# Last phase of a decoder block on one core: each full-height matmul replaced by two of 64 rows into separate banks

## The chip, the cores and the metric

One core of one Trainium2 chip runs the whole program. The metric is the device time of one execution in microseconds (us), the median of several runs. Below, a *product* is one matmul of TensorE whose moving operand has 512 columns (or the two half-height ones that take its place), and a *unit* is 256 rows by 512 columns of a weight matrix (512 KB): two tiles of 128 rows, used with two blocks of 128 tokens in three passes, so 12 products.

## The reference

One layer of a hybrid block: x (256 tokens, width 2048, float32) is RMS-normalised and projected by one wide matrix (2048 x 18432) to the inputs of two token mixers, a retention and a differential attention, and their gates. Then:

```
o_ret  = rmsnorm(retention(rq, rk, rv)) * silu(rz)
o_diff = rmsnorm(diff_attention(dq, dk, dv)) * (1 - lam_init) * silu(dz)
mixed  = sigmoid(g_ret) * (o_ret @ w_ret_up) + sigmoid(g_diff) * (o_diff @ w_diff_up)
h      = x + mixed @ w_out
out    = rmsnorm(h) * final_norm_w
```

All of it is float32. The last phase, which the change concerns, is `o_diff @ w_diff_up`, the merge into `mixed`, `mixed @ w_out`, the sum with x and the final norm.

## The kernel before

**Products.** Float32 accuracy comes from splitting each operand into a rounded part (`_hi`) and a remainder (`_lo`), both of the type fp32r, and adding three passes: hi x hi, hi x lo, lo x hi (`three_passes`, lines 1218 to 1224). The activations are the stationary operand (128 rows of the contraction by 128 tokens), the weights are the moving one (128 rows by 512 columns). A group is 512 output columns for both token blocks: 8 units, 16 contraction tiles, accumulated in two banks of PSUM (one for each token block). `start_group` waits until both banks have been drained.

**The stream of weights.** Units are numbered through the whole program; the ring for them has 4 slots. For each unit SP loads it into `raw` (line 397), when the slot's last remainder has been computed; ScalarE rounds it into `w_hi` (line 562), when TensorE is done with the slot; VectorE subtracts, giving `w_lo` (line 806); TensorE waits for both at the start of the unit (`units_split`). ScalarE and VectorE run three units ahead, in loops over `s` written out by hand: at each step first the split of unit s + 3, then whatever else the step has.

**Last phase.** 64 units: four groups g = 0 to 3 with `w_diff_up` and `ot` as the stationary operand, then four groups g = 4 to 7 with `w_out` and `xt`. `tail_banks` gives the groups banks 2, 3 and 0, 1 by turns. At the first step behind each of the groups 0 to 3 VectorE runs `merge_diff` (line 1092): it multiplies the gate by each bank (line 1098) and adds that to `mixed` (line 1102). One step later it transposes the two results in squares of 32 (line 821); SP moves the strips with 8 DMAs (`turn`, line 405), which stand in its queue ahead of a load of weights; three steps later ScalarE rounds the result into `xt_hi` (line 759) and VectorE takes the remainder `xt_lo` (line 1115). TensorE needs the last quarter of that operand at the seventh unit (u = 6) of group 4, line 1334. Behind the last rounding ScalarE issues two loads, x again into `gate` and the final norm's weights into `zs` (lines 780, 781). Behind each of the groups 4 to 6 VectorE adds the banks to x (`add_residual`, line 1123), the first time after waiting for these loads; the split of the unit follows behind it in the queue at the next step. ScalarE squares and sums the rows, GpSimd multiplies by the final weights.

**The end.** In the last group the last four units are taken block by block (line 1341), so that block 0's final chain (add, squares, reciprocal root on GpSimd, scaling, store) runs under block 1's products, and block 1's stands behind them.

**The start.** TensorE's program begins with nine semaphore increments (line 1179), then waits for a tile of ones and runs nine warm-up matmuls on it (line 1251), then the first products, `tile_by_pass` (line 1188). The first unit comes in halves of one tile each: ScalarE rounds the second half at line 639.

Of the kernel before, what the change touches and what calls it, by code (L numbers as in the profile page):

```python
# [31 lines left out]
P = 128  # L32
# [13 lines left out]
AHEAD = 3  # L46
GROUPS_D = D // COLS
HALF = COLS // 2

QK = 128  # L50
V = 256
# [29 lines left out]
SQUARE = 32  # L81
STRIPS = P // SQUARE
TURN = 16 * STRIPS
WARM_UPS = 9
TURN_LAG = AHEAD + RING + 1


# [52 lines left out]
def diff_uses_high(it, j):  # L140
    return it * 4 + (9 + j)
# [14 lines left out]

def tail_uses_low(j):
    return 19 + j


def tail_banks(g):

    return 2 - 2 * (g % 2)
# [8 lines left out]
def build(nc, x, x_t, norm_w, w_in, w_ret_up, w_diff_up, w_out, lambda_q1, lambda_k1, lambda_q2,  # L172
# [5 lines left out]
    with ExitStack() as ctx:  # L178
# [3 lines left out]
        def sem(name):  # L182
            return ctx.enter_context(nc.semaphore(name))
# [106 lines left out]
        mt_hi_ready = sem("mt_hi_ready")  # L290
        x_again = sem("x_again")
        h_ready = sem("h_ready")
        h_squared = sem("h_squared")
        h_weighted = sem("h_weighted")
        h_norm_step = sem("h_norm_step")
# [10 lines left out]
        def lam_row(i):  # L306

            return gate[:, 1, i * P:(i + 1) * P]

        def attn_of(a):  # L310

# [485 lines left out]
        def _(dve):  # L797
# [294 lines left out]
            def merge_diff(j):  # L1092

                group_done(U_TAIL + (j + 1) * UNITS - 1)
                cols = slice(j * COLS, (j + 1) * COLS)
                banks = tail_banks(j)
                for b in range(BLOCKS):
                    dve.tensor_tensor(gate[:, b, cols], gate[:, b, cols], bank[banks + b][:, :], ALU.mult) \
                       .then_inc(drained[banks + b], 1)
                for b in range(BLOCKS):  # L1100
                    dve.wait_ge(drained[banks + b], tail_uses_low(j // 2) + 1)
                    dve.tensor_tensor(mixed[:, b, cols], mixed[:, b, cols], gate[:, b, cols], ALU.add) \
                       .then_inc(mixed_ready, 1)
# [15 lines left out]
            def add_residual(j, b):  # L1119

                cols = slice(j * COLS, (j + 1) * COLS)
                bk = tail_banks(j) + b
                dve.tensor_tensor(gate[:, b, cols], gate[:, b, cols], bank[bk][:, :], ALU.add).then_inc(h_ready, 1)  # L1123

                dve.wait_ge(h_ready, 2 * j + b + 1)
                dve.sem_inc(drained[bk], 1)

            for s in range(FIRST, 2 * GROUPS_D * UNITS):
                if U_TAIL + s + AHEAD < U_END:
# [46 lines left out]

        @block.tensor
        def _(pe):
            pe.sem_inc(units_done, RING)
            for b in range(8):  # L1180
                pe.sem_inc(filled[b], 1)

            def start_group(banks, uses):

                for b in range(BLOCKS):
                    pe.wait_ge(drained[banks + b], uses)
# [31 lines left out]
            def three_passes(s, u, kk, bk, b, left_hi, left_lo):  # L1218

                k = u * KU + kk  # L1220
                hi, lo = left_hi[:, k, b * P:(b + 1) * P], left_lo[:, k, b * P:(b + 1) * P]
                pe.matmul(bank[bk][:, :], hi, w_hi[:, s, kk, :], start=k == 0, stop=False)  # L1222
                pe.matmul(bank[bk][:, :], hi, w_lo[:, s, kk, :], start=False, stop=False)  # L1223
                return pe.matmul(bank[bk][:, :], lo, w_hi[:, s, kk, :], start=False, stop=k == KT - 1)  # L1224

            def keys_by_v(dst, a, x, b, v_col, start, stop):

                hi, lo = keys_hi(a)[:, x * P:(x + 1) * P], keys_lo(a)[:, x * P:(x + 1) * P]
                cols = slice(v_col, v_col + V)
                pe.matmul(dst, hi, v_hi[:, b, cols], start=start, stop=False)  # L1230
                pe.matmul(dst, hi, v_lo[:, b, cols], start=False, stop=False)  # L1231
                return pe.matmul(dst, lo, v_hi[:, b, cols], start=False, stop=stop)  # L1232
# [12 lines left out]
                pe.matmul(dst, left_hi[:, m, left], right_lo[:, m, right], start=False, stop=False)  # L1245
                return pe.matmul(dst, left_lo[:, m, left], right_hi[:, m, right], start=False, stop=True)  # L1246


            pe.wait_ge(ones_ready, 1)
            for i in range(WARM_UPS):  # L1250
                pe.matmul(bank[7][:, 0:P], ones[:, :], ones[:, :], start=True, stop=True)  # L1251

            for it in range(RET_ITS):
                n0 = it * (RET_G * UNITS) + U_RET
# [71 lines left out]
            for s in range(2 * GROUPS_D * UNITS - RING):  # L1326
                g, u = s // UNITS, s % UNITS
                banks = tail_banks(g)
                if u == 0:
                    start_group(banks, tail_uses_low(g // 2))  # L1330
                if g == 0 and u in (0, 6):
                    pe.wait_ge(ot_lo_ready, 2 * HEADS - 2 + 2 * (u // 6))
                if g == GROUPS_D and u in (0, 6):
                    pe.wait_ge(mt_lo_ready, 2 * GROUPS_D - 2 + 2 * (u // 6))
                if g < GROUPS_D:
                    unit(U_TAIL + s, u, banks, ot_hi, ot_lo)
                else:
                    unit(U_TAIL + s, u, banks, xt_hi, xt_lo)


            for b in range(BLOCKS):
                for u in range(UNITS - RING, UNITS):
                    if b == 0:
                        pe.wait_ge(units_split, 2 * (U_END - UNITS + u + (RING + 1)))
                    for kk in range(KU):
                        mm = three_passes(u % RING, u, kk, tail_banks(GROUPS_D - 1) + b, b, xt_hi, xt_lo)
                mm.then_inc(filled[tail_banks(GROUPS_D - 1) + b], 1)


# [53 lines left out]
```

## Time and profile before

| | |
|---|---|
| median of 3 runs | 1092.63 us (1092.34 to 1092.67) |
| the profiled execution | 1092.4 us |
| its span in the profile | 1090.6 us |
| mean granted TensorE clock | 0.997 of full speed |
| busy: matmuls / weight loads / VectorE / ScalarE / GpSimd | 1080.7 / 900.1 / 686.7 / 528.1 / 47.2 us |

PE is TensorE's matmul row, PEld its loads of the stationary operand (they overlap matmuls), DVE is VectorE, ACT ScalarE, POOL GpSimd, SP SyncE; a q behind a name is the engine's sequencer, where DMAs are issued. The profile's matmul rows give a length of 0.39 us for a product, but products follow each other faster than that, since they are pipelined and their ends are modelled: their pace is read from the starts. L1222 is line 1222 of the kernel. In a row of the timeline, what stands in brackets is the idle time of the engine before it and what ended it.

### The profile page before, as it was taken

How to read it: one execution, taken by the hardware profiler on the slowest of the kernel's cores; microseconds unless marked ns; L12 is line 12 of the kernel's file. 1: busy time of each engine (PE TensorE's matmuls, PEld its weight loads, DVE VectorE, ACT ScalarE, POOL GpSimd, SP SyncE). 2: the span in 40 equal slices, each digit the busy share in tenths (PEclk: the TensorE clock that was granted, in tenths of full speed). 3: DMA queues.
4: the chain of work that ended last, by engine and by line, in shares of the span. 5: the costliest groups of instructions: out<-in, count | busy, mean ns of one | idle time of the engine just before them, and what ended most of it. 6: DMA issues, size and time to landing. Idle time of an engine off the chain costs nothing.

```text
span 1090.6 us, 13145 instructions
## 1 busy us (share of the span) xinstructions
PE 1080.7 (99%) x4890; PEld 900.1 (83%) x4890; DVE 686.7 (63%) x848; ACT 528.1 (48%) x689; POOL 47.2 (4%) x63
## 2 busy tenths in 40 slices
PE   9999999999999999999999999999999999999997
PEld 7888888888888888888888888888888888888885
DVE  6675575485566455566766767576757676676554
ACT  6554455344455433344654464446544554444443
POOL 0100000000000000000100002000200020000111
PEclk9999999999999999999999999999999999999998
DMA  9877667666667655667566766766677666666862
GB/s 326 305 245 219 182 196 209 193 199 209 193 181 212 201 195 194 192 179 245 167 216 186 219 200 196 213 200 196 205 209 213 195 205 201 208 211 211 323 213 101
DMA packets 141072, 227.97 MB, mean 209 GB/s; under 512 B 14416, under 2 KB 40784, under 8 KB 140240
## 3 DMA queue, kind: packets, MB, share of 16 engines
q1 hardware_dynamic: 140448, 223.98, 66.3%
q10 hardware_dynamic: 560, 3.15, 0.7%
q8 instruction: 38, 0.62, 0.2%
q14 instruction: 26, 0.21, 0.1%
HBM read 210.84 MB, written 2.10 MB: 195 GB/s over the span
## 4 chain that ended last, share of the span: by engine, by line
PE 99%; issue 1%; DVE 0%; POOL 0%; ACT 0%; ACTq 0%; POOLq 0%; DVEq 0%
PE bank L1222 31%; PE bank L1223 31%; PE bank L1224 31%; PE bank L1232 1%; PE bank L1231 1%; PE bank L1230 1%; PE bank L1251 0%; PE bank L1194 0%; PE bank L1198 0%; PE bank L1201 0%; PE bank L1313 0%; PE bank L1246 0%; PE bank L1245 0%; PE bank L1244 0%; PE bank L1270 0%
## 5 line engine op out<-in xcount | busy, mean ns | idle before, releaser
L806 DVE TENSOR_TENSOR w_lo<-raw,w_hi 128x1024 fp32r<-128x1024 f32 x380 | 471.0, 1244 | 372.1 <-ACT w_hi L562 371.0
L562 ACT ACTIVATE w_hi<-raw 128x1024 fp32r<-128x1024 f32 x380 | 402.9, 1061 | 521.4 <-PE bank L1224 487.8
L1222 PE MATMUL bank<-w_hi,xt_hi 128*128 128x512 f32 x1264 | 493.1, 390 | 0.0
L1224 PE MATMUL bank<-w_hi,xt_lo 128*128 128x512 f32 x1264 | 491.9, 389 | 0.0
L1223 PE MATMUL bank<-w_lo,xt_hi 128*128 128x512 f32 x1264 | 491.8, 389 | 0.0
L1224 PEld LDWEIGHTS bank<-w_hi,xt_lo 128*128 128x128 f32 x1264 | 237.3, 188 | 49.6
L1222 PEld LDWEIGHTS bank<-w_hi,xt_hi 128*128 128x128 f32 x1264 | 237.3, 188 | 48.8
L1223 PEld LDWEIGHTS bank<-w_lo,xt_hi 128*128 128x128 f32 x1264 | 237.4, 188 | 48.5
L1222 PE MATMUL bank<-w_hi,ot_hi 128*128 128x512 f32 x256 | 99.6, 389 | 0.0
L1223 PE MATMUL bank<-w_lo,ot_hi 128*128 128x512 f32 x256 | 99.6, 389 | 0.0
L1224 PE MATMUL bank<-w_hi,ot_lo 128*128 128x512 f32 x256 | 99.6, 389 | 0.0
L1222 PEld LDWEIGHTS bank<-w_hi,ot_hi 128*128 128x128 f32 x256 | 48.0, 188 | 10.0
L1223 PEld LDWEIGHTS bank<-w_lo,ot_hi 128*128 128x128 f32 x256 | 48.0, 188 | 10.0
L1224 PEld LDWEIGHTS bank<-w_hi,ot_lo 128*128 128x128 f32 x256 | 48.0, 188 | 9.9
L531 POOL TENSOR_TENSOR zs<-zs,sub 128x512 f32<-128x512 f32 x8 | 14.1, 1787 | 498.9 <-DVE zs L871 498.9
L842 DVE TENSOR_TENSOR rot<-rot 128x512 f32<-128x512 f32 x24 | 16.6, 693 | 2.5
L821 DVE STREAM_TRANSPOSE squares_t<-rot 128x512 f32<-128x512 f32 x24 | 17.1, 711 | 0.8
L541 POOL TENSOR_TENSOR mixed<-gate,zs 128x512 f32<-128x512 f32 x6 | 10.6, 1788 | 160.0 <-DVE gate L1123 160.0
L516 POOL TENSOR_TENSOR ms<-ss,eps_sb 128x2 f32<-128x2 f32 x16 | 5.1, 322 | 279.8 <-ACT junk L596 279.8
L833 DVE TENSOR_TENSOR rot<-bank,rope_sb 128x512 f32<-128x512 f32 x24 | 16.4, 683 | 0.6 <-POOL rope_sb L510 0.6
L836 DVE TENSOR_TENSOR rot<-bank,rope_sb 128x512 f32<-128x512 f32 x24 | 16.3, 679 | 0.0
L738 ACT ACTIVATE probs<-probs,neg_max 128x256 f32<-128x256 f32 (+1 forms) x32 | 14.1, 443 | 0.7 <-DVE neg_max L1054 0.7
(112 smaller groups left out, 474.8 us busy)
## 6 DMA issues: line engine op xcount, KB each, us to landing
raw<-w_in_dram SPq DMA_DIRECT2D x284, 512.0 KB, 4.3
raw<-w_ret_up_dram SPq DMA_DIRECT2D x32, 512.0 KB, 3.6
raw<-w_diff_up_dram SPq DMA_DIRECT2D x32, 512.0 KB, 4.5
raw<-w_out_dram SPq DMA_DIRECT2D x32, 512.0 KB, 4.5
rot<-squares_t SPq DMA_DIRECT2D x96, 64.0 KB, 2.4
zs<-squares_t SPq DMA_DIRECT2D x48, 64.0 KB, 2.2
normed<-squares_t SPq DMA_DIRECT2D x48, 64.0 KB, 2.2
raw<-w_in_dram SPq DMA_DIRECT2D x8, 256.0 KB, 5.3
```

What stands on the lines that cost most here:

```text
L531: pool.tensor_tensor(z, z, sub08[:, :].unsqueeze(1).broadcast_to([P, 2, V]), ALU.mult) \
L562: act.activation(w_hi[:, s, :, :], raw[:, s, :, :], ACT.Copy).then_inc(hi_ready, 1)
L738: last = act.activation(p, p, ACT.Exp, bias=neg_max[:, a, j:j + 1], accum_out=row_sum[:, a, j:j + 1])
L806: dve.tensor_tensor(w_lo[:, s, :, :], raw[:, s, :, :], w_hi[:, s, :, :].bitcast(F32), ALU.subtract) \
L821: dve.transpose(to, src).then_inc(squares_ready[slot], 1)
L833: dve.tensor_tensor(rot[:, 0, :].rearrange("p (g d) -> p g d", d=64), src[:, :].rearrange("p (g d) -> p g d", d=64), cos, ALU.mult) \
L836: dve.tensor_tensor(rot[:, 1, :].rearrange("p (m s d) -> p m s d", s=2, d=64), src[:, :].rearrange("p (m s d) -> p m s d", s=2, d=64)[:, : ...
L842: dve.tensor_tensor(rot[:, 0, :], rot[:, 0, :], rot[:, 1, :], ALU.add).then_inc(rot_ready, 1)
L1222: pe.matmul(bank[bk][:, :], hi, w_hi[:, s, kk, :], start=k == 0, stop=False)
L1223: pe.matmul(bank[bk][:, :], hi, w_lo[:, s, kk, :], start=False, stop=False)
L1224: return pe.matmul(bank[bk][:, :], lo, w_hi[:, s, kk, :], start=False, stop=k == KT - 1)
L1230: pe.matmul(dst, hi, v_hi[:, b, cols], start=start, stop=False)
```

## The change

In the last phase each product becomes two (`row_halves`): the lower 64 rows of both operands into the banks 0 to 3 as before, the upper 64 rows into the bank four further up (`UPPER`), one after the other in TensorE's program. The two partial sums are added by VectorE: in `merge_diff` the lower bank is copied to SBUF, the upper is added, and the gate is multiplied by that; in `add_residual` the two banks are added one after the other. Each of these steps waits for the one before it. The banks 4 to 7, which the last phase did not use before, are guarded by `tail_uses_upper`. Separately, the warm-up matmuls are eight instead of nine and stand ahead of the nine increments. No other phase is changed.

```diff
-WARM_UPS = 9
+WARM_UPS = 8
+HALF_P = P // 2
+UPPER = 4
...
+def tail_uses_upper(g):
+    return diff_uses_high(DIFF_ITS - 1, 4) + g // 2 if g % 2 == 0 else 1 + g // 2
...
+        def rows_sum(b):
+            return probs[:, b * COLS:(b + 1) * COLS]
...
@@ merge_diff
                 for b in range(BLOCKS):
-                    dve.tensor_tensor(gate[:, b, cols], gate[:, b, cols], bank[banks + b][:, :], ALU.mult) \
+                    dve.tensor_copy(rows_sum(b), bank[banks + b][:, :]).then_inc(row_sums, 1)
+                    dve.wait_ge(row_sums, 4 * j + 2 * b + 1)
+                    dve.tensor_tensor(rows_sum(b), rows_sum(b), bank[UPPER + banks + b][:, :], ALU.add).then_inc(row_sums, 1)
+                    dve.wait_ge(row_sums, 4 * j + 2 * b + 2)
+                    dve.sem_inc(drained[UPPER + banks + b], 1)
+                    dve.tensor_tensor(gate[:, b, cols], gate[:, b, cols], rows_sum(b), ALU.mult) \
                        .then_inc(drained[banks + b], 1)
...
@@ add_residual
-                dve.tensor_tensor(gate[:, b, cols], gate[:, b, cols], bank[bk][:, :], ALU.add).then_inc(h_ready, 1)
+                dve.tensor_tensor(gate[:, b, cols], gate[:, b, cols], bank[bk][:, :], ALU.add).then_inc(h_lower, 1)
+                dve.wait_ge(h_lower, 2 * j + b + 1)
+                dve.sem_inc(drained[bk], 1)
+                dve.tensor_tensor(gate[:, b, cols], gate[:, b, cols], bank[UPPER + bk][:, :], ALU.add).then_inc(h_ready, 1)
 
                 dve.wait_ge(h_ready, 2 * j + b + 1)
-                dve.sem_inc(drained[bk], 1)
+                dve.sem_inc(drained[UPPER + bk], 1)
...
@@ tensor engine
+            pe.wait_ge(ones_ready, 1)
+            for i in range(WARM_UPS):
+                pe.matmul(bank[7][:, 0:P], ones[:, :], ones[:, :], start=True, stop=True)
+
             pe.sem_inc(units_done, RING)
             for b in range(8):
                 pe.sem_inc(filled[b], 1)
...
+            def row_halves(s, u, kk, bk, b, left_hi, left_lo):
+
+                k = u * KU + kk
+                tokens = slice(b * P, (b + 1) * P)
+                for left, right, first, last in ((left_hi, w_hi, k == 0, False), (left_hi, w_lo, False, False),
+                                                 (left_lo, w_hi, False, k == KT - 1)):
+                    pe.matmul(bank[bk][:, :], left[0:HALF_P, k, tokens], right[0:HALF_P, s, kk, :], start=first, stop=last)
+                    mm = pe.matmul(bank[UPPER + bk][:, :], left[HALF_P:P, k, tokens], right[HALF_P:P, s, kk, :], start=first,
+                                   stop=last)
+                return mm
+
+            def unit_by_rows(n, u, banks, left_hi, left_lo):
+
+                pe.wait_ge(units_split, 2 * n + (2 * RING + 2))
+                for kk in range(KU):
+                    for b in range(BLOCKS):
+                        mm = row_halves(n % RING, u, kk, banks + b, b, left_hi, left_lo)
+                mm.then_inc(units_done, 1)
...
-            pe.wait_ge(ones_ready, 1)
-            for i in range(WARM_UPS):
-                pe.matmul(bank[7][:, 0:P], ones[:, :], ones[:, :], start=True, stop=True)
...
                 if u == 0:
                     start_group(banks, tail_uses_low(g // 2))
+                    start_group(UPPER + banks, tail_uses_upper(g))
...
                 if g < GROUPS_D:
-                    unit(U_TAIL + s, u, banks, ot_hi, ot_lo)
+                    unit_by_rows(U_TAIL + s, u, banks, ot_hi, ot_lo)
                 else:
-                    unit(U_TAIL + s, u, banks, xt_hi, xt_lo)
+                    unit_by_rows(U_TAIL + s, u, banks, xt_hi, xt_lo)
...
-                        mm = three_passes(u % RING, u, kk, tail_banks(GROUPS_D - 1) + b, b, xt_hi, xt_lo)
+                        mm = row_halves(u % RING, u, kk, tail_banks(GROUPS_D - 1) + b, b, xt_hi, xt_lo)
```

## Rows read from the trace of the kernel before

**Rows 1.** The page, busy us of each engine (share of the span) and instructions.

```profile
PE 1080.7 (99%) x4890; PEld 900.1 (83%) x4890; DVE 686.7 (63%) x848; ACT 528.1 (48%) x689; POOL 47.2 (4%) x63
```

**Rows 2.** The page, the chain that ended last, by engine.

```profile
PE 99%; issue 1%; DVE 0%; POOL 0%; ACT 0%; ACTq 0%; POOLq 0%; DVEq 0%
```

**Rows 3.** Windows: busy us of each engine (instructions), in two stretches of the phase.

```profile
915.00:1000.00 85.00, 85.00 (x376) 70.38 (x375) 53.98 (x60) 36.39 (x38) 0.00 (x0) 1.00 0.65 213
1000.00:1083.00 83.00, 82.89 (x366) 68.32 (x364) 45.78 (x50) 35.36 (x45) 11.14 (x7) 1.00 0.59 209
```

**Rows 4.** Timeline (start us, length us), last phase, two products 12 apart.

```profile
950.13 0.39 PE L1222 MATMUL bank<-w_hi,ot_hi 128*128 128x512 f32 x1
...
952.85 0.39 PE L1222 MATMUL bank<-w_hi,ot_hi 128*128 128x512 f32 x1
```

**Rows 5.** Timeline of TensorE's matmuls, products of 256 columns, five apart.

```profile
894.31 0.28 PE L1230 MATMUL bank<-v_hi,ot_hi 128*128 128x256 f32 x1
...
894.91 0.28 PE L1232 MATMUL bank<-v_hi,ot_lo 128*128 128x256 f32 x1
```

**Rows 6.** Timeline of the start, the first real products.

```profile
5.99 0.93 PE L1194 MATMUL bank<-w_hi,xt_hi 128*128 128x512 f32 x2
6.49 0.63 ACT L639 ACTIVATE w_hi<-raw 128x512 fp32r<-128x512 f32 x1 [1.46 <-DMA raw<-w_in_dram]
...
7.45 0.41 PEld L1194 LDWEIGHTS bank<-w_hi,xt_hi 128*128 128x128 f32 x2
```

**Rows 7.** Timeline of the end, last group.

```profile
1077.49 0.69 DVE L1123 TENSOR_TENSOR gate<-gate,bank 128x512 f32<-128x512 f32 x1 [2.78 <-PE bank L1224]
...
1078.37 0.43 DVE L1158 CUSTOM_DVE_ANT_0 mixed<-gate 128x256 f32<-128x256 f32 x1 [0.18 <-DVE gate L1123]
...
1080.03 0.49 DVE L1172 TENSOR_SCALAR mixed<-mixed,h_rstd 128x512 f32<-128x512 f32 x1 [0.73 <-POOL h_rstd L545]
...
1082.51 0.39 PE L1224 MATMUL bank<-w_hi,xt_lo 128*128 128x512 f32 x1
1082.93 0.69 DVE L1123 TENSOR_TENSOR gate<-gate,bank 128x512 f32<-128x512 f32 x1 [1.75 <-PE bank L1224]
```

**Rows 8.** Timeline of the weight loads, where products have 128 columns.

```profile
865.06 0.54 PEld L1313 LDWEIGHTS bank<-zs,left_whole 128*128 128x128 f32 x4
865.52 0.19 PEld L1222 LDWEIGHTS bank<-w_hi,xt_hi 128*128 128x128 f32 x1
```

**Rows 9.** Timeline of VectorE, last phase.

```profile
968.88 1.23 DVE L806 TENSOR_TENSOR w_lo<-raw,w_hi 128x1024 fp32r<-128x1024 f32 x1 [0.24 <-ACT w_hi L562]
...
998.20 1.28 DVE L1098 TENSOR_TENSOR gate<-gate,bank 128x512 f32<-128x512 f32 x2
...
1000.60 1.22 DVE L806 TENSOR_TENSOR w_lo<-raw,w_hi 128x1024 fp32r<-128x1024 f32 x1
...
1009.92 1.29 DVE L1115 TENSOR_TENSOR xt_lo<-rot,xt_hi 128x512 fp32r<-128x512 f32 x2 [0.76 <-ACT xt_hi L759]
...
1024.18 1.52 DVE L1123 TENSOR_TENSOR gate<-gate,bank 128x512 f32<-128x512 f32 x2 [2.92 <-DMA zs<-final_norm_w_dram]
1025.92 1.81 DVE L806 TENSOR_TENSOR w_lo<-raw,w_hi 128x1024 fp32r<-128x1024 f32 x1 [0.22 <-DVE gate L1123]
```

**Rows 10.** Timeline of TensorE's matmuls, the first products of three units.

```profile
973.93 0.39 PE L1222 MATMUL bank<-w_hi,ot_hi 128*128 128x512 f32 x1
...
1012.01 0.39 PE L1222 MATMUL bank<-w_hi,xt_hi 128*128 128x512 f32 x1
...
1028.33 0.39 PE L1222 MATMUL bank<-w_hi,xt_hi 128*128 128x512 f32 x1
```

**Rows 11.** Timeline of ScalarE and its queue, behind the last rounding.

```profile
1009.50 0.39 ACTq L780 DMA_DIRECT2D gate<-x_dram  x1
```

**Rows 12.** The chain that ended last at the start (start us, us, what).

```profile
0.93 1.23 issue
2.16 4.18 PE bank L1251 x18
```

More of the change, by code:

```diff
@@ L292, in build @@
         h_ready = sem("h_ready")
+        h_lower = sem("h_lower")
+        row_sums = sem("row_sums")
         h_squared = sem("h_squared")
```

## The prediction

> **What bounds the kernel now.** Four views, in this order. The page's busy shares: TensorE's matmul row is at 99% of the span [rows 1], but the ends of matmuls are modelled, so this alone says little. The chain that ended last is 99% TensorE and 1% issue [rows 2]: the array is the bound, everywhere. The windows over the last phase (64 units of 12 products, 768 in all) show matmuls filling 85.00 of 85.00 us and 82.89 of 83.00, VectorE at 54.0 and 45.8 [rows 3]: VectorE has room on average, TensorE has none. The timeline then gives the period of a product: the one at 950.13 and the one at 952.85 are 12 apart, 2.72 us, 0.2267 each [rows 4]. Products of 256 columns follow each other by (894.91 - 894.31) / 5 = 0.120 us [rows 5]. The 256 further columns cost 0.1067 us, so 512 cost 0.2133, and each change of the stationary operand about 13.3 ns, whatever the width. Work that is not hidden by products lies at the two ends only: 5.99 us before the first real one [rows 6], and 1090.6 - (1082.51 + 0.39) = 7.7 us behind the last one's end [rows 7].
>
> **1. The 768 products become 1536 of half height.** Their arithmetic doesn't shrink: each half still streams 512 columns, 0.2133 us. All that can be won is the 13.3 ns, 768 x 0.0133 = 10.2 us, and only if one half's change hides under the other half's stream, and the other way round, without lengthening the period of either. Against this: each half is a chain of its own (stream, change, stream), and its period stays 0.2133 + 0.0133 however the other one is placed in time. Two such chains side by side end when one does. I take no change, 0.2267 us for a pair.
>
> Bound below: 0.2133, that is -10.2 us. Bound above: the loads, of which each pair needs two. Where products are narrow (128 columns) loads set the pace: four take 0.54 us from the first's start to the last's end, one 0.19, so they start (0.54 - 0.19) / 3 = 0.117 us apart [rows 8]. Two loads one after the other are 0.233 us, against the 0.2267 that hide them: the cover that was wide (one load in 0.2267) is used up. At 0.233 a pair costs 6.7 ns more, 5.1 us over 768. The far bound: the halves do not run side by side at all, 768 x 0.2267 = +174 us. The nearest rows, the periods and the loads, lie within 6% of 0.2267 on both sides; that value is taken.
>
> A rule of the Trainium skill speaks against the change here: "TensorE: Matmul & The Clock Gate", section "LDWEIGHTS (loading the stationary operand)", has the load's time go by columns and not by rows, so a load of 64 rows costs what one of 128 does. By its figure, an estimate of 107 ns each, two would just fit under a product, and the sum would stay as it is. No load of 64 rows is in this trace. "TensorEngine Tiling (Array Packing)", section "Tiling Modes", speaks for the change: tiles load and multiply independently. By it the halves do run side by side, and perhaps their loads too; the trace of before shows neither.
>
> **2. VectorE's merge, four times.** Before: two multiplications from the banks and two additions, from 998.20 to the next operation's start at 1000.60, 2.40 us, 0.60 apiece, since they overlap [rows 9]. After, per block: copy, wait, add the upper bank, wait, multiply. A step that needs the one before it starts 0.88 us after it (1077.49 to 1078.37 [rows 7]), against 0.60 for an independent one. The copy from a bank is not in the trace: its nearest rows are the 0.49 us scaling [rows 7] and the multiplication from a bank, 1.28 - 0.60 = 0.68 us [rows 9]; I take the latter, which reads a bank too. A block costs 0.88 + 0.88 + 0.60 = 2.36 instead of 0.60, +1.76 (1.35 to 1.8 with a short copy and short waits); two blocks, rounded down, +3.4 us (2.7 to 3.6).
>
> Behind it, in the same queues, stand the transpositions, the eight DMAs of the turn on SP, ScalarE's rounding, VectorE's remainder, and the splits of the next units' weights. The path is one line, so all of it comes 3.4 us later.
> - After the second merge, the split of unit 24 ended at 968.88 + 1.23 = 970.1 [rows 9]; TensorE starts that unit at 973.93 [rows 10]. 3.4 later it still fits, by 0.4. After the first and the third, where the turn's DMAs land sooner, more than 1 us is left. Cost nothing.
> - After the fourth, the output product needs the last quarter of its stationary operand at its unit 6. That remainder was ready at 1009.92 + 1.29 = 1011.2 [rows 9]; unit 6 starts at 1012.01 [rows 10]. Slack 0.8. With +3.4 it is there at 1014.6: TensorE waits **2.6 us** (1.9 to 2.8).
> - ScalarE issues the reload of x and of the final weights behind its rounding, at 1009.50 [rows 11]; they go 3.4 us later. The residual sum of the first output group waits for them until 1024.18 (VectorE idle 2.92), and behind it in VectorE's queue the split of unit 12 of the output product ends at 1025.92 + 1.81 = 1027.7 [rows 9], with the unit at 1028.33 [rows 10]. Slack 0.6.
>
> **3. The residual sum, four times.** Four additions, two of them dependent, instead of two. Before, two take 1025.92 - 1024.18 = 1.74 us with their waits [rows 9], so +1.75. For the first group this adds to the late reload: 3.4 + 1.75 - 0.6 = 4.5 us late at unit 12, of which 2.6 are waited already. The reload (3072 KB in 14.7 us, with some four weight transfers of 512 KB among it) now meets one of these fewer, since SP sends it ahead: up to 1.5 us at that rate, of which I take 0.5. Both waits together **4.0 us** (2.5 to 5.0). The later groups don't wait for a reload: nothing.
>
> **4. The end.** The second block's chain of the last group starts behind TensorE's last product, with the addition at 1082.93 [rows 7]. One more dependent addition stands in it: **+0.9 us** (0.7 to 0.9). The first block's chain was at its scaling at 1080.03, with one operation to go; 0.9 later it is still out of the way.
>
> **5. The start.** The nine increments ahead of the warm-up stand in 1.23 us of issue between 0.93 and 2.16, and the 18 records of warm-up take 4.18 us, 0.23 apart against 0.117 for the same shape later [rows 8, 12]: half clock. They hold the first real product until 5.99. Freed, and one warm-up (2 records, 0.46 us) shorter, TensorE could start at about 4.7. But the second half's rounding runs from 6.49 to 7.12, and TensorE came to it at 7.45 already [rows 6]: **-0.3 us**. The other way: if the array stayed at half clock up to 1.5 us longer than it did, 3 to 4 products more at twice the period, +0.8. Nobody waits for the increments, which now lie under the warm-up, before 7 us.
>
> **Sum.** The profiled execution took 1092.4 us (1.8 outside the span of 1090.6): 0 + 4.0 + 0.9 - 0.3 = +4.6, 1097.0. The median of the runs shown, 1092.63, is 0.2 above it and gives 1097.2; I say 1097. The case's own range is 1095 to 1099.5.
>
> **Rivals.**
> A. *The change of operand hides.* For: the excess is the same at 512 and 256 columns, so it may sit in something that the other half can use the time of. Against: the argument of the two chains. Price: the waits above are set by VectorE and count from the start of the output product, so unit 12 comes at the same time whatever the period: the 12 units before it save nothing, 52 x 12 x 0.0133 = 8.3 us is saved, less 0.9 at unit 24, whose slack of 0.4 goes when eight units run 1.3 us faster. 1097.2 - 8.3 + 0.9 = 1089.8. It gives "faster" when over nine tenths of the excess vanish, or when the waits are at their low end.
> B. *Loads set the pace*, 0.233 us a pair: 52 x 12 x 0.0067 = +4.2 us, 1101.4. For: the spacing of loads. Against: those loads waited for products as well, and might go closer.
> C. *The halves run partly or not side by side*, the change doesn't do what it says: from 0.25 us a pair (52 x 12 x 0.0233 = +14.6, 1111.8) to one after the other (1267). For: no row shows two products in the array from different rows. Against: only that it would be possible.
> D. *VectorE's extra time is covered.* Were the merge only 0.8 us longer there would be no wait at all, and the sum is +0.6, 1093.2. Against: three operations can't take the time of one.
>
> **Chances.** Forecast 0.36, A 0.30, B 0.12, C 0.13, D 0.09. A measurement of this kernel can tell some 0.2% from no change, 2.2 us: 1090.4 to 1094.8. A is 0.20 faster and 0.10 within; D 0.02 faster and 0.07 within; 0.04 of the forecast is within. Faster 0.22, same 0.21, slower 0.57. The range 1087.5 to 1106 leaves out C and the far end of A.
>
> **What would show it.** The period of a pair in the timeline: 0.227 is the forecast, 0.213 to 0.216 A, 0.233 B, more C. A gap in TensorE ahead of the seventh unit of the output product, with mt's remainder at its end, about 2.6 us, and one before unit 12, about 1.4: steps 2 and 3; neither: D. VectorE from the merge's first operation to the split behind it: 5.8 us instead of 2.4. From TensorE's last product to the end: 0.9 more. First real product at 4.7, second tile at 7.1 to 7.2: step 5. The forecast is wrong if a pair's period is off by over 4 ns, or if no wait stands at unit 6.

## The result, and the profile after

The changed kernel takes **1103.03 us** (median of 4 runs, 1101.64 to 1103.64) against 1092.58 for the kernel before in the same measurement: a ratio of 1.0094, 95% interval [1.0082, 1.0106]. It is slower, as forecast, and inside the wide range (1087.5 to 1106), but outside the 1095 to 1099.5 that the forecast gave for its own case: it loses 10.4 us where the forecast of 1097 meant 4.4. The profiled execution took 1101.64 us with a span of 1099.8, so span against span the change cost 9.2 us, and that is the difference which the traces can take apart. The last phase's 64 units are numbered 0 to 63 here; a group has eight. The output product starts at unit 32, so its "unit 6" and "unit 12" are units 38 and 44. The fourth merge stands behind group 3, and its place is told from the start of unit 32.

First the page: busy us of each engine, and the chain that ended last [rows 1, 2].

```profile
PE 1084.9 (99%) x5656; PEld 903.4 (82%) x5656; DVE 703.4 (64%) x872; ACT 529.0 (48%) x689; POOL 44.5 (4%) x63
```

```profile
PE 91%; DMA 3%; DVE 2%; SPq 1%; issue 1%; ACT 1%; ACTq 0%; POOLq 0%; POOL 0%; DVEq 0%
```

TensorE's share hardly moved, but its part of the chain fell from 99% to 91%: the path to the end now leaves the array for a DMA, VectorE and SyncE's queue. The busy line would not have told that.

**The period.** TensorE and its loads in the timeline (start, length), one product and the two behind it [rows 4]:

```profile
959.72 0.39 PE L1257 MATMUL bank<-w_hi,ot_hi 64*128 64x512 f32 x1
959.73 0.39 PE L1258 MATMUL bank<-w_hi,ot_hi 64*128 64x512 f32 x1
...
960.18 0.39 PE L1257 MATMUL bank<-w_hi,ot_lo 64*128 64x512 f32 x1
...
960.18 0.18 PEld L1257 LDWEIGHTS bank<-w_hi,ot_hi 64*128 64x128 f32 x1
960.18 0.18 PEld L1258 LDWEIGHTS bank<-w_hi,ot_hi 64*128 64x128 f32 x1
...
960.40 0.39 PE L1257 MATMUL bank<-w_hi,ot_hi 64*128 64x512 f32 x1
```

A pair every (960.40 - 959.72) / 3 = 0.2267 us, as before to the last digit. The two halves start within 0.01 us of each other, and so do their two loads: the loads are not one after the other, which rival B needed. The Trainium skill ("TensorE: Matmul & The Clock Gate", section "The mechanism") has the products of tiles in different rows start about 4 ns apart and their loads run beside products in flight; the trace agrees, with 0.01 us between the halves in the rows above. A load of 64 rows takes 0.18 us here, one of 128 rows 0.19 [rows 8]. In the Trainium skill (same page, section "LDWEIGHTS (loading the stationary operand)") the time of a load goes by its columns and not by its rows; the trace agrees, though these rows are longer than the 107 ns that the prediction estimated from that page.

**VectorE in the fourth merge** [rows 9], timeline:

```profile
1000.64 0.68 DVE L1111 COPY probs<-bank 128x512 f32<-128x512 f32 x1
1001.36 0.69 DVE L1113 TENSOR_TENSOR probs<-probs,bank 128x512 f32<-128x512 f32 x1
1002.19 0.69 DVE L1116 TENSOR_TENSOR gate<-gate,probs 128x512 f32<-128x512 f32 x1
...
1006.16 1.22 DVE L819 TENSOR_TENSOR w_lo<-raw,w_hi 128x1024 fp32r<-128x1024 f32 x1
```

The merge lasts from 1000.64 to 1006.16, 5.52 us instead of 2.40: +3.12, where +3.4 was forecast. But it also *starts* late: 1000.64 against 998.20 before, 2.44 us, of which TensorE's own schedule explains only 0.60 (unit 32 starts at 996.29, before at 995.69). It begins 4.35 us behind the start of unit 32 instead of 2.51. That 1.84 is nobody's price in the forecast.

**TensorE at the two waits** [rows 10], timeline:

```profile
1017.59 0.79 PE L1257 MATMUL bank<-w_hi,xt_hi 64*128 64x512 f32 x1 [4.42 <-DVE xt_lo L1133]
...
1018.61 0.63 PE L1257 MATMUL bank<-w_hi,xt_lo 64*128 64x512 f32 x1
1019.03 0.63 PE L1257 MATMUL bank<-w_hi,xt_hi 64*128 64x512 f32 x1
...
1036.61 0.50 PE L1257 MATMUL bank<-w_hi,xt_hi 64*128 64x512 f32 x1 [0.84 <-DVE w_lo L819]
```

Unit 38 starts 7.30 us after unit 37 instead of 2.72. Behind the wait the pairs come 0.42 us apart, not 0.227: the windows over that stretch (columns: window, its length, busy us of PE, PEld, DVE, ACT, POOL, granted clock, DMA share, GB/s) show why.

```profile
1017.60:1021.00 3.40, 3.40 (x16) 2.74 (x18) 1.34 (x2) 1.13 (x2) 0.00 (x0) 0.51 1.04 399
1021.10:1024.50 3.40, 3.40 (x33) 2.81 (x31) 2.16 (x2) 1.06 (x1) 0.00 (x0) 1.00 1.00 407
```

A granted clock of 0.51 is the lower of the two levels. It lasts 3.4 us behind an idle stretch of 4.42, and unit 38 takes 1.67 us longer for it (4.39 instead of 2.72).

**The chain through unit 12** (start, us, what), from the turn behind the fourth merge to TensorE [rows 11 for the reload]:

```profile
1007.30 0.72 DVE squares_t L834
1008.08 0.55 SPq L418
...
1012.57 2.92 DMA rot<-squares_t
...
1015.78 0.39 ACTq L793
1016.19 14.69 DMA zs<-final_norm_w_dram
1030.90 0.70 DVE gate L1141
...
1034.31 2.25 DVE w_lo L819
1036.61 0.50 PE bank L1257
```

Read it as one line: transposition, eight DMAs, their landing, ScalarE's issue of the reload, 14.7 us of transfer, the residual sum, the split, TensorE. Nothing in it is the array. A delay of the fourth merge arrives at unit 12 in full, less the slack of 0.6, as long as the transfers behind it keep their lengths.

**ScalarE behind the first turn**, timeline. These rows show how lateness is handed on:

```profile
947.09 1.16 ACT L772 ACTIVATE xt_hi<-rot 128x512 fp32r<-128x512 f32 x2 [4.46 <-DMA rot<-squares_t]
...
950.25 1.06 ACT L575 ACTIVATE w_hi<-raw 128x1024 fp32r<-128x1024 f32 x1 [1.05 <-DMA raw<-w_diff_up_dram]
951.58 1.06 ACT L575 ACTIVATE w_hi<-raw 128x1024 fp32r<-128x1024 f32 x1 [0.27 <-DMA raw<-w_diff_up_dram]
952.85 1.06 ACT L575 ACTIVATE w_hi<-raw 128x1024 fp32r<-128x1024 f32 x1 [0.21 <-DMA raw<-w_diff_up_dram]
```

VectorE next to it:

```profile
951.41 3.83 DVE L819 TENSOR_TENSOR w_lo<-raw,w_hi 128x1024 fp32r<-128x1024 f32 x3 [0.89 <-ACT w_hi L575]
955.16 0.69 DVE L1111 COPY probs<-bank 128x512 f32<-128x512 f32 x1
```

ScalarE stands 4.46 us before the strips (1.33 in the trace of before), then waits for weights; three roundings come close together, VectorE splits three units in a row, and only then can the second merge begin. In the trace of before ScalarE had caught up with the array by then and waited for it. The four merges start 0.1, 0.5, 2.0 and 2.4 us later than before.

The chain that ended last (start, us, what) shows the same links further on, from the second merge's transposition to the fourth merge:

```profile
961.82 0.72 DVE squares_t L834
...
968.84 4.59 DMA raw<-w_diff_up_dram
...
973.51 1.07 ACT w_hi L575
...
985.10 0.72 DVE squares_t L834
...
991.64 5.32 DMA raw<-w_out_dram
...
997.05 1.07 ACT w_hi L575
...
999.50 1.23 DVE w_lo L819
1000.72 0.61 DVE probs L1111
```

The transposition lets the turn's DMAs go. The load behind them in SyncE's queue lands and is rounded, three splits run in a row, and the third merge starts right behind the last of them, as VectorE's timeline has it:

```profile
974.68 3.84 DVE L819 TENSOR_TENSOR w_lo<-raw,w_hi 128x1024 fp32r<-128x1024 f32 x3 [0.78 <-ACT w_hi L575]
978.43 0.68 DVE L1111 COPY probs<-bank 128x512 f32<-128x512 f32 x1
```

The merge lasts to 983.96, a split follows, and the third transposition stands at 985.10; behind its turn comes the next load, and behind the splits of that one the fourth merge. None of these steps is TensorE's. (Between 977.24 and 985.10 the profile's own chain goes by another load and leaves 0.54 us unexplained; the merge and the split fill that time on VectorE.)

**End and start.** VectorE at the end [rows 7], and TensorE's products at the start of the first unit's two tiles [rows 6]:

```profile
1091.34 0.69 DVE L1141 TENSOR_TENSOR gate<-gate,bank 128x512 f32<-128x512 f32 x1 [0.91 <-PE bank L1258]
1092.17 0.69 DVE L1144 TENSOR_TENSOR gate<-gate,bank 128x512 f32<-128x512 f32 x1
```

```profile
4.92 1.19 PE L1219 MATMUL bank<-w_hi,xt_hi 128*128 128x512 f32 x2 [0.16 <-ACT w_hi L647]
...
7.41 0.66 PE L1219 MATMUL bank<-w_hi,xt_hi 128*128 128x512 f32 x2
```

The first six products follow each other at 0.42 us here, (7.41 - 4.92) / 6, and before at 0.28 (the second tile's first product stood at 7.67): of the 1.07 us by which the first product starts earlier, 0.26 are left at the second tile.

The ledger, from the starts of the units' first products:

| where | before | after | costs |
|---|---|---|---|
| start of unit 0 | 908.65 | 908.57 | -0.08 |
| unit 0 to 32: first change to half height 0.16, small waits 0.52 | 87.04 | 87.72 | +0.68 |
| unit 32 to 44 | 32.64 | 40.32 | +7.68 |
| unit 44 to the last product (0.13 behind the wait) | 54.18 | 54.30 | +0.12 |
| last product to the end of the span | 8.09 | 8.92 | +0.83 |
| span | 1090.6 | 1099.8 | +9.2 |

### The profile page after: what moved, and what is told of

Read it like the earlier page. It is cut to its first block, busy times and chain, and to the rows that moved or that the text cites. A ratio compares the mean times of both kernels' runs of the same rounds, so it can differ in the third digit from the quotient of the medians.

```text
span 1099.8 us, 14725 instructions
## 1 busy us (share of the span) xinstructions
PE 1084.9 (99%) x5656; PEld 903.4 (82%) x5656; DVE 703.4 (64%) x872; ACT 529.0 (48%) x689; POOL 44.5 (4%) x63
## 4 chain that ended last, share of the span: by engine, by line
PE 91%; DMA 3%; DVE 2%; SPq 1%; issue 1%; ACT 1%; ACTq 0%; POOLq 0%; POOL 0%; DVEq 0%
PE bank L1249 26%; PE bank L1248 26%; PE bank L1247 26%; PE bank L1257 9%; DMA zs<-final_norm_w_dram 1%; SPq L418 1%; DMA raw<-w_diff_up_dram 1%; DVE w_lo L819 1%; PE bank L1276 1%; PE bank L1275 1%; PE bank L1274 1%; DMA raw<-w_out_dram 0%; PE bank L1219 0%; ACT w_hi L575 0%; PE bank L1223 0%
## 5 line engine op out<-in xcount | busy, mean ns | idle before, releaser
L1247 PE MATMUL bank<-w_hi,xt_hi 128*128 128x512 f32 x1136 | 443.3, 390 | 0.0
L1248 PE MATMUL bank<-w_lo,xt_hi 128*128 128x512 f32 x1136 | 442.0, 389 | 0.0
L1257 PE MATMUL bank<-w_hi,xt_hi 64*128 64x512 f32 x128 | 50.5, 395 | 5.3 <-DVE xt_lo L1133 4.4
L1258 PE MATMUL bank<-w_hi,xt_hi 64*128 64x512 f32 x128 | 50.6, 395 | 0.0
L1257 PE MATMUL bank<-w_lo,xt_hi 64*128 64x512 f32 x128 | 50.0, 391 | 0.0
L1258 PE MATMUL bank<-w_lo,xt_hi 64*128 64x512 f32 x128 | 50.0, 391 | 0.0
L1258 PE MATMUL bank<-w_hi,xt_lo 64*128 64x512 f32 x128 | 49.9, 390 | 0.0
L1257 PE MATMUL bank<-w_hi,xt_lo 64*128 64x512 f32 x128 | 49.9, 390 | 0.0
L1247 PE MATMUL bank<-w_hi,ot_hi 128*128 128x512 f32 x128 | 49.8, 389 | 0.0
L1248 PE MATMUL bank<-w_lo,ot_hi 128*128 128x512 f32 x128 | 49.8, 389 | 0.0
L1249 PE MATMUL bank<-w_hi,ot_lo 128*128 128x512 f32 x128 | 49.8, 389 | 0.0
L1258 PE MATMUL bank<-w_hi,ot_hi 64*128 64x512 f32 x128 | 49.8, 389 | 0.0
L1257 PE MATMUL bank<-w_hi,ot_hi 64*128 64x512 f32 x128 | 49.8, 389 | 0.0
L1257 PE MATMUL bank<-w_lo,ot_hi 64*128 64x512 f32 x128 | 49.4, 386 | 0.0
L1258 PE MATMUL bank<-w_lo,ot_hi 64*128 64x512 f32 x128 | 49.4, 386 | 0.0
```

Source lines behind the costliest of these rows:

```text
L1257: pe.matmul(bank[bk][:, :], left[0:HALF_P, k, tokens], right[0:HALF_P, s, kk, :], start=first, stop=last)
L1258: mm = pe.matmul(bank[UPPER + bk][:, :], left[HALF_P:P, k, tokens], right[HALF_P:P, s, kk, :], start=first, stop=last)
```

## The experiments

All ratios are against the kernel before on the same chip.

**1. The halves without VectorE's work** (start as before):

```
-  unit(U_TAIL + s, u, banks, ...)
+  unit_by_rows(U_TAIL + s, u, banks, ...)
   # merge and residual sum as before, on the lower banks
```

> Kernel after, but VectorE's merge and residual sum are those of before and read the lower banks alone (the upper partial sums are computed and left out of the result), and the start is that of before. Theory 1 (all of the loss is VectorE's lateness): no waits, pairs every 0.2267 us, +0.2 us for the 0.16 seen once in the first unit. Rival (the half-height stream itself costs: the array's change of division, twice the instructions, twice the loads): several of the 10.4 us are here.

Measured: 1092.83 us, ratio 1.0001 [0.9991, 1.001]. TensorE never waits in the last phase, every unit takes 2.72 us; only unit 0 takes 2.88, the same 0.16 as in the kernel after. The array's part of the change costs nothing and gives nothing.

**2. VectorE's work without the halves** (each bank read twice, so the values are not the reference's):

```
+  dve.tensor_copy(rows_sum(b), bank[banks + b])      # then add the same bank, then multiply
+  dve.tensor_tensor(gate, gate, bank[bk], ALU.add)   # the residual's bank once more
```

> Kernel before, full-height products and start of before; only VectorE has the longer merge (copy, add, multiply, each waiting) and the longer residual sum, on the one bank there is, which is read twice (so the sums are not the reference's). Theory 1: +10 us, with the same 4.6 us wait at unit 6 of the output product and the same 3.4 us of half clock behind it. Rival: clearly less, because halves and VectorE's work disturb each other.

Measured: 1100.81 us, 1.008 [1.0065, 1.0095]. That is +8.1 where +10 was expected, but most of the loss is here, with products of full height. Unit 38 comes 3.33 late and unit 44 another 2.29; this time the clock fell behind the second wait (2.1 us) and stayed up behind the first (3.2 us).

**3. The start alone**, in two runs of the same kernel:

```
-WARM_UPS = 9
+WARM_UPS = 8        # and the warm-up ahead of the increments
```

> Kernel before with eight warm-ups ahead of the increments and nothing else. By the prediction -0.3 us; by the trace after, in which the last phase begins 0.08 us earlier, -0.1 us. Rival: the slower start of the array (more products at half clock) costs 0.5 us or more in other executions and explains part of the spread of the runs after.

> The kernel of e3 once more, in more rounds: whether the start alone beats the kernel before. By e3, -0.8 us (0.08%); by the profile after, -0.1; by the prediction, -0.3.

Measured: 1091.9 us, 0.9994 [0.9984, 1.0004], and 1091.84, 0.9993 [0.9984, 1.0002]: -0.8 and -0.7, each time not told from no change. Unit 0 starts at 907.85 and 908.41, before at 908.65. In all eight traces with this start it lies between 907.85 and 908.72, in the seven with the start of before between 908.36 and 909.37: some 0.5 us earlier on the average, by ranges that overlap.

**4. Only the fourth merge made longer**, on the kernel before:

```
+LONG = lambda j: j == GROUPS_D - 1    # copy, add, multiply in this merge alone
```

> Kernel before with the longer merge only behind group 3 (bank read twice). Theory 1 (lateness carries over from merge to merge, 2.4 us of it were there ahead of the fourth): without the first three the fourth is 3.1 us late, TensorE waits 3.1 - 0.8 = 2.3 us at unit 6 and, through the late reload, 0.2 more ahead of unit 12: +2.5 us, as the prediction had it for this part, and the clock stays up. Rival (the fourth merge alone does it, by a slower turn of the strips): a wait of 4 us or more and the clock falls, +7 us.

Measured: 1095.27 us, 1.0028 [1.0016, 1.004], +2.5. TensorE's waits show one place in the last phase (us, times, longest):

```profile
PE bank L1238 <- DVE xt_lo L1131: 2.0, 1, 2.0
```

The wait is 2.0 where 2.3 was expected, and unit 44 comes 2.43 late. The forecast's arithmetic for a merge is right, if that merge is the only long one. The clock stays at 1.00 behind this wait.

**5. All merges long but the fourth**, on the kernel after (the fourth merge and so its group leave out the upper sums):

```
+  if j == GROUPS_D - 1:
+      dve.tensor_tensor(gate, gate, bank[banks + b], ALU.mult); continue
```

> Kernel after, but the merge behind group 3 is that of before (two multiplications, on the lower banks alone; that group's upper sums are left out of the result). Theory 1 (lateness is handed from merge to merge by the queue of loads): this merge still begins 2.4 us late; TensorE waits 4.6 - 3.1 = 1.5 us at unit 6 instead of 4.6, the reload is 3.1 us earlier, and the whole is 3.1 us shorter than after: about +6 to +7 us over before. Rival (no carry-over, the fourth merge's own length made it): the wait at unit 6 is gone and +2 us over before.

Measured: 1098.22 us, 1.0053 [1.0038, 1.0068]. VectorE's timeline at the fourth merge:

```profile
1000.16 1.28 DVE L1113 TENSOR_TENSOR gate<-gate,bank 128x512 f32<-128x512 f32 x2
...
1002.56 1.22 DVE L819 TENSOR_TENSOR w_lo<-raw,w_hi 128x1024 fp32r<-128x1024 f32 x1
```

The short merge again takes 2.40 us, but it starts at 1000.16 with unit 32 at 995.85: 4.31 behind it, as in the kernel after (4.35), where the kernel before has 2.51. So 1.8 us of the lateness at the fourth merge come from the three before it, which the forecast had called free. The time is below the +6 to +7 that was expected: from unit 32 to 44 it is 4.0 us shorter than after, not 3.1, since the turn (8.29 us, after 8.48) and the reload (14.48, after 15.12) were shorter too.

**6. The wait at unit 38 filled** with 16 idle products, on the kernel after:

```
+  for i in range(FILLERS):
+      pe.matmul(bank[0], xt_hi[:, 0, 0:P], xt_hi[:, 0:2, :], start=True, stop=True)
```

> Kernel after with 16 idle products into a free bank ahead of the wait at unit 6 of the output product, so that the array doesn't stand still there. Theory 1: the clock stays up and unit 6 runs in 2.7 instead of 4.4 us, but unit 12 is held by VectorE's residual sum behind the late reload, so its wait grows from 1.0 to 2.7 us and the time stays that of after (within 0.5 us). Rival: the half clock is a loss of its own, 1.7 us shorter than after.

Measured: 1104.49 us, 1.0104 [1.0084, 1.0123]: +11.9 where the kernel after has +10.4, with intervals that overlap. TensorE's timeline at the two places:

```profile
1019.47 0.50 PE L1258 MATMUL bank<-w_hi,xt_hi 64*128 64x512 f32 x1 [0.75 <-DVE xt_lo L1134]
...
1039.36 0.79 PE L1258 MATMUL bank<-w_hi,xt_hi 64*128 64x512 f32 x1 [3.28 <-DVE w_lo L820]
```

With the idle gap only 0.75 the clock stays up at unit 38, which takes 2.85 us instead of 4.39. But unit 44 then waits 3.28, and there the clock falls. From unit 32 to unit 44 it takes 42.02 us, after 40.32: nothing is won, and 1.70 more is lost. The rows say why. In this execution the fourth merge began 4.97 us behind unit 32 (after 4.35), and the reload took 16.05 us from issue to use (after 15.12). From that use to unit 44 it is 5.66 us, after 5.71: unit 12 comes when the reload lets it, at either clock. The 1.67 of half clock in the kernel after was hidden under that wait, and a remedy for the clock there would have gained nothing.

**7. The lower halves alone** (a single run; the upper products and sums are left out, the start is that of before):

> As e1, but the upper halves' matmuls are left out altogether (half the arithmetic of the last phase isn't done). Theory 1 (each half is a chain of its own: stream of 512 columns, then the change of operand): a half alone follows its predecessor by 0.2267 us too, the last phase is as long as in e1, 1092.8 us. Rival (the period is set by the pair, by two loads or two streams sharing something): a half alone is quicker, 0.2133 to 0.22 us, 5 to 10 us less.

Measured: 1093.51 us in one run, span 1091.5. TensorE, timeline, two products three apart:

```profile
958.26 0.39 PE L1245 MATMUL bank<-w_hi,ot_lo 64*128 64x512 f32 x1
...
958.94 0.39 PE L1245 MATMUL bank<-w_hi,ot_lo 64*128 64x512 f32 x1
```

Half of the array, alone, takes 0.227 us a product: half the rows, the same period. That is what a chain of its own for each half gives, with the excess over 0.2133 in each. What the excess consists of no run here shows.

**8 and 9. The turn's DMAs out of SyncE's queue**, on the kernel after: the strips issued by GpSimd, or by ScalarE. They ask whether the loads standing behind the turn hand the lateness on.

```
-  turn_mixed(j, b)                          # SyncE
+  pool.dma_start(rot strip, squares_t)      # 8: GpSimd;   9: act.dma_start(...)
```

> Kernel after, but in the last phase GpSimd, idle there, issues the strips' DMAs instead of SP, so that no load of weights stands behind a wait for VectorE's transposition. Theory 1 (the handing on goes through SP's queue): splits no longer come in threes behind each merge, the fourth merge begins within 0.5 us of its place in before (998.2), TensorE's small waits (0.9 us in all ahead of unit 6) are gone; 1 to 3 us shorter than after, unless GpSimd issues more slowly than SP's 0.63 us apiece, which would show as later rounding on ScalarE. Rival (it goes through VectorE's own queue): the fourth merge is still 2 us late or more.

> Kernel after, but ScalarE's queue issues the strips' DMAs of the last phase, between its splits of units 6 and 7 of each group; it would wait for them there anyway. SP issues only loads of weights. Theory 1b (the lateness is handed on by loads that stand behind the turn in SP's queue, after e8, where the turn itself became 3 us slower, left this open): splits behind the rounding no longer wait for loads, the fourth merge begins within 0.5 us of its place relative to TensorE in before (2.5 us behind the group's start, against 4.35 in after), and the time is 2 us or more below after. Rival (it is ScalarE's own wait for the strips, in order, that piles up the splits, whoever issues them): the fourth merge is still 1.5 us late or more and the time as after.

Measured: 1108.99 us, 1.0154 [1.0137, 1.017], and 1107.7, 1.0142 [1.0128, 1.0156]. Both expectations missed: the time is 5 to 6 us above that of the kernel after. In experiment 9 the four roundings behind the first turn follow each other with no wait for a load (951.03 to 954.92). But ScalarE's queue is taken for 5.58 us by the issuing, the strips take 4.6 us from issue to landing (median, after 2.5) with SyncE's loads going on beside them, and the first rounding of a turned result comes at 949.98 instead of 947.09. The fourth merge starts at 1005.45 and at 1004.83, where the kernel after has 1000.64. It is 3.18 us behind unit 32 in both, instead of 4.35, but that is no measure of what is handed on: TensorE itself waited at units 16, 24 and 32, and takes 93.85 and 93.08 us from unit 0 to unit 32 (after 87.72). So the two runs don't tell how much of the 1.84 passes through the loads' place behind the turn; the chain shown above passes there. The turn in SyncE's queue, ahead of the loads, was the best of the three places.

**10. The reload ahead of the last rounding**, on the kernel after:

```
-  if g == GROUPS_D and u == 5:
+  if g == GROUPS_D and u == 4:      # ahead of read_mt_hi
```

> Kernel after, but ScalarE issues the reload of x and the final weights ahead of its last rounding instead of behind it. Theory 1: unit 12 no longer waits (1.1 us) and the time falls by about 1 us if the strips' DMAs are not slowed by the reload; if they are, the wait at unit 6 grows by as much as they come later, and the time stays or rises. Rival (the late reload is what holds everything): 4 us or more below after.

Measured: 1107.49 us, 1.0138 [1.0124, 1.0152]. ScalarE:

```profile
1006.69 0.39 ACTq L790 DMA_DIRECT2D gate<-x_dram  x1
...
1021.67 1.15 ACT L772 ACTIVATE xt_hi<-rot 128x512 fp32r<-128x512 f32 x2 [13.93 <-DMA rot<-squares_t]
```

The wait at unit 44 is gone, and 3072 KB in front of the strips put 10.9 us of waiting at unit 38. Of these two orders the one of the kernel after is the better.

**11. Only the residual sum longer**, on the kernel before:

```
+  dve.tensor_tensor(gate, gate, bank[bk], ALU.add).then_inc(h_lower, 1)
+  dve.wait_ge(h_lower, 2 * j + b + 1)
```

> Kernel before with only the residual sums longer (each bank is added twice, one addition waiting for the other). By the prediction's steps 3 and 4: 1.7 - 0.6 = 1.1 us of wait ahead of unit 12 and 0.8 at the end, +1.9 us. Rival (the wait ahead of unit 12 exists only because the merges are late): +0.8 us.

Measured: 1095.02 us, 1.0023 [1.0013, 1.0033], +2.5. TensorE's wait:

```profile
PE bank L1230 <- DVE w_lo L812: 1.4, 1, 1.4
```

1.51 us come at unit 44 where 1.1 was expected, 0.72 at the end. The difference is not in the sum itself (3.19 us, so 1.45 more than before) but in the split behind it: this one operation takes 2.32 us, before 1.81 [rows 9] (1.79 in experiment 4). Experiments 4 and 11, each part alone, add up to +5.0, near the forecast's 4.9 for both; but each of the two uses the slack of 0.6 for itself, which one kernel has only once, so that the nearness is partly luck.

**12. Experiment 2 with spare increments**, so that VectorE's queue is that of the kernel after, instruction by instruction:

```
+  dve.sem_inc(spare, 1)      # where the kernel after frees an upper bank
```

> As e2, with a semaphore increment between the addition and the multiplication of each merge and between the two additions of each residual sum, where the kernel after has one (on a semaphore that nobody waits for). Theory 1 (the increments make the dependent step 0.11 us later, 0.2 a merge, and the lateness that is handed on grows with it): the fourth merge begins 4.2 to 4.4 us behind the group's start as in after (e2: 3.7), +9.5 to +10.5 us. Rival (halves and VectorE's work disturb each other): +8, as e2.

Measured: 1101.38 us, 1.0075 [1.0058, 1.0092]. VectorE in the fourth merge, which starts at 1001.14:

```profile
1001.86 0.69 DVE L1110 TENSOR_TENSOR probs<-probs,bank 128x512 f32<-128x512 f32 x1
1002.69 0.69 DVE L1113 TENSOR_TENSOR gate<-gate,probs 128x512 f32<-128x512 f32 x1
```

and TensorE at unit 38:

```profile
1017.34 0.50 PE L1243 MATMUL bank<-w_hi,xt_hi 128*128 128x512 f32 x1 [3.62 <-DVE xt_lo L1133]
```

Without one product of half height this trace repeats the kernel after: span 1099.7 against 1099.8, the fourth merge 4.25 behind unit 32, as expected, the clock at its lower level for 3.4 us in unit 38, small waits at units 24 to 37. The median, +8.7, lies below the +9.5 to +10.5 that was expected and above the rival's +8.

The kernels side by side, in us between the starts of units (as in the ledger):

| kernel | 0 to 32 | 32 to 38 | 32 to 44 | last product to end | median - before |
|---|---|---|---|---|---|
| before | 87.04 | 16.32 | 32.64 | 8.09 | |
| 1 halves only | 87.19 | 16.32 | 32.64 | 8.09 | +0.1 |
| 4 fourth merge | 87.04 | 18.49 | 35.07 | 8.09 | +2.5 |
| 11 residual | 87.04 | 16.32 | 34.15 | 8.82 | +2.5 |
| 5 after, fourth short | 87.64 | 17.95 | 36.30 | 8.93 | +5.6 |
| 2 all VectorE work | 87.04 | 19.65 | 38.41 | 8.81 | +8.1 |
| 12 the same, increments | 87.56 | 20.45 | 39.52 | 8.95 | +8.7 |
| after | 87.72 | 21.30 | 40.32 | 8.92 | +10.4 |

## Why the prediction was right in kind and wrong in size

**Step 1 held.** The pair's period is 0.2267 us, and experiment 7 fits the reason given, two chains side by side. Rivals A (0.2133), B (0.233) and C (above) are refuted by the period and by experiment 1. Rival D falls with the wait at unit 38. (The far end of C, 1267, is 1092.6 + 174 and leaves out the forecast's own waits.)

**Step 4 held** (+0.83 for 0.9). **Step 5** is within what moves the start from one execution to the next: -0.08 in the trace, -0.8 and -0.7 in medians that don't tell it from nothing. The first real product came at 4.92 (forecast 4.7). The 7.45 that the forecast took for the second tile is the row of its load; in the kernel after that load stands at 7.34, not at 7.1 to 7.2, since the products ahead of it went at 0.42 us: that is the forecast's own counter-case, an array that stays slow for longer.

**Step 2 failed, in two of its sentences.** The size of one merge was right (3.12 for 3.4), and experiment 4 confirms what it does alone. Wrong was "The path is one line, so all of it comes 3.4 us later", and with it, of the second merge, "3.4 later it still fits, by 0.4 ... Cost nothing". Each merge was priced against the schedule of before, as if the last one had not been late. The forecast looked only at whether TensorE's next unit was in time; the lateness was not paid there, but carried in the ring of weights: turn late, loads behind it late, roundings and splits in a burst, next merge late. Experiment 5 shows the 1.8 us with a short fourth merge, and the rows from 961.82 to 1000.72 show the way. That SyncE's queue alone carries it is not shown: experiments 8 and 9 changed too much else. The small waits at units 24 to 37 (0.92 in all) are the same lateness where it first shows, since that slack of 0.4 was used up.

**Steps 2 and 3 at unit 12.** Forecast: 4.0 us for both waits. Measured from unit 32 to unit 44: 7.68. The difference of 3.7, from the rows: 1.84 handed on; 0.71 because the turn takes longer (transposition to reload 1007.30 to 1015.78, 8.48 us; before 7.77); 0.94 because the reload took 15.1 us from issue to use where 14.7 less 0.5 was taken (the three loads behind the turn move with it, 1013.97 to 1015.15, before 1007.63 to 1009.19, so that the reload meets seven loads in either kernel and not one fewer); -0.28 and -0.08 for the merge (3.12 for 3.4) and the residual sum (1030.90 to 1034.31, 3.41 for 1.74, so 1.67 for 1.75). So step 3's "now meets one of these fewer, since SP sends it ahead" failed too. That makes 3.1; of the rest, some 0.5, 0.43 lie in the split behind the residual sum, which takes 2.24 us instead of 1.81 (experiment 11 has 2.32 with that sum alone made longer). GpSimd multiplies beside it in both kernels; why it is longer is not shown. The half clock behind unit 38, which the forecast did not have, is no further term: experiment 6. The other 0.9 of the span's difference from the forecast are the 0.68 ahead of unit 32, the 0.12 behind unit 44 and the 0.2 by which the start fell short, less 0.07 at the end.

**What stays open.** By spans the VectorE work alone (experiment 12) gives +9.1 of the +9.2. By medians it gives +8.7 against +10.4, with intervals that overlap only at their ends ([1.0058, 1.0092] and [1.0082, 1.0106]). The runs of either kernel spread over 2 us or more, and the profiled execution of the kernel after was its fastest. What is handed on varies too: experiments 6 and 10 have the same program as the kernel after up to the fourth merge, and it starts 4.97 and 4.67 us behind unit 32 in their traces, so 1.8 to 2.5 us over the 2.51 of before. Whether the half products add a microsecond in the executions that were not profiled is not settled. No version here beats the kernel before by more than the measurement tells.

## What to carry to other kernels

Splitting a product of full height by rows gained nothing here, where the array was kept busy: each half kept the whole product's period, and the second set of banks had to be added up by somebody. When a step recurs, price its second occurrence from the state that the first one leaves, not from the trace of before; a slack is spent once, and a ring that is refilled behind the late step hands the rest on. And before an unexpected stall or clock drop is put on the bill, ask whether the next wait on the path would have taken the time anyway.

## What the runs showed of the hardware

- Two products from different rows of the array, into different banks, start within 0.01 us in a steady stream, and their loads too. The first unit of half height takes 0.16 us more, once (kernel after and experiment 1).
- VectorE: a step that needs the one before it starts 0.72 us behind it (128x512, from a bank or not), 0.83 where a semaphore increment of its own stands between them (experiments 2 and 12); the forecast took 0.88.
- The granted clock fell to the lower level for some 3.4 us behind waits of 4.4 and 3.6 us at unit 38 (after, experiment 12) and of 3.3 and 2.1 at unit 44 (experiments 6 and 2), but not behind 3.2 (experiment 2) and 2.0 (experiment 4) at unit 38. The length of the wait alone does not decide it in these runs.
- Strips of 64 KB land in 2.5 us (median) when SyncE issues them ahead of its weight loads (kernel after), and in 4.6 when ScalarE issues them and SyncE's loads go on (experiment 9).
